# Cutting the POOL subtraction of each weight unit into two instructions of 512 columns in place of four of 256

## The reference

```
def swiglu(h, w_in, w_out):
    gate, up = jnp.split(h @ w_in, 2, axis=-1)
    return (jax.nn.silu(gate) * up) @ w_out
...
        x = x + 0.5 * swiglu(rms_norm(x, norm_ffn1_w[l]), ffn1_w_in[l], ffn1_w_out[l])
        x = x + hybrid_mixer(rms_norm(x, norm_mix_w[l]), w_in_mix[l], conv_w[l], conv_b[l], ...)
        x = x + memory_cross_attention(rms_norm(x, norm_cross_w[l]), rms_norm(mem, norm_mem_w[l]), ...)
        x = x + 0.5 * swiglu(rms_norm(x, norm_ffn2_w[l]), ffn2_w_in[l], ffn2_w_out[l])
```

## Time and profile before

| | |
|---|---|
| median of 3 runs | 2134.8 us (2134.48 to 2135.26) |
| span of the profiled execution | 2133.4 us, first to last instruction |
| PE busy | 2114.8 us, 99% |
| DVE busy | 829.8 us, 39% |
| ACT busy | 803.6 us, 38% |
| POOL busy | 1120.5 us, 53% |
| `w_lo` instructions on POOL | 1448 of 128x256, mean 783 ns |
| granted PE clock | 1.000 of full speed |

### The profile page before, as it was taken

The page is one execution under the profiler, slowest core; times in us unless marked ns, Lnnn a source line. Parts: engine busy times, 40 slices in busy tenths (PEclk is TensorE's granted clock), DMA queues, the critical chain, the costliest instruction groups (busy, mean ns, idle before and its releaser), DMA issues.

```text
span 2133.4 us, 29164 instructions
## 1 busy us (share of the span) xinstructions
PE 2114.8 (99%) x10122; PEld 1740.7 (82%) x10122; DVE 829.8 (39%) x1489; ACT 803.6 (38%) x1345; POOL 1120.5 (53%) x1493
## 2 busy tenths in 40 slices
PE   9999999999999999999999999999999999999999
PEld 7888888878887778877888888887787888888887
DVE  5222211762841766143322222208744474023244
ACT  5222232325834655323322223326554343122233
POOL 6555555673354337725655555554545466555554
PEclk9999999999999999999999999999999999999999
DMA  6322233233322213412332223321222223332322
GB/s 214 119 98 98 99 106 106 85 99 96 114 99 79 75 55 122 155 40 89 99 98 98 95 94 117 99 96 63 79 89 79 89 80 108 99 99 99 99 89 80
DMA packets 61344, 207.71 MB, mean 97 GB/s; under 512 B 6616, under 2 KB 8088, under 8 KB 61256
## 3 DMA queue, kind: packets, MB, share of 16 engines
q1 hardware_dynamic: 55216, 195.84, 27.8%
q10 hardware_dynamic: 6040, 10.65, 1.5%
HBM read 204.31 MB, written 4.77 MB: 98 GB/s over the span
## 4 chain that ended last, share of the span: by engine, by line
PE 42%; issue 28%; POOL 27%; DVE 2%; POOLq 0%; ACT 0%; DMA 0%; SPq 0%; DVEq 0%; ACTq 0%
POOL w_lo L463 27%; PE bank L516 11%; PE bank L518 11%; PE bank L517 11%; PE bank L678 1%; PE bank L680 1%; PE bank L679 1%; PE bank L908 1%; PE bank L932 1%; PE bank L840 1%; PE bank L920 0%; DVE gx_lo L2394 0%; DVE bank L2403 0%; PE bank L846 0%; DVE x L2405 0%
## 5 line engine op out<-in xcount | busy, mean ns | idle before, releaser
L463 POOL TENSOR_TENSOR w_lo<-w_raw,w_hi 128x256 fp32r<-128x256 f32 x1448 | 1087.1, 783 | 933.4 <-ACT w_hi L1283 933.3
L516 PE MATMUL bank<-gx_hi,w_hi 128*128 128x512 f32 (+1 forms) x1768 | 674.9, 382 | 7.8 <-DVE gx_lo L2394 4.5
L518 PE MATMUL bank<-gx_hi,w_lo 128*128 128x512 f32 (+1 forms) x1768 | 668.1, 378 | 0.0
L517 PE MATMUL bank<-gx_lo,w_hi 128*128 128x512 f32 (+1 forms) x1768 | 667.6, 378 | 0.0
L1283 ACT CAST w_hi<-w_raw 128x1024 fp32r<-128x1024 f32 x364 | 378.4, 1045 | 347.9 <-PE bank L518 291.8
L516 PEld LDWEIGHTS bank<-gx_hi,w_hi 128*128 128x128 f32 x1768 | 332.6, 188 | 74.2 <-DVE gx_lo L2394 6.4
L518 PEld LDWEIGHTS bank<-gx_hi,w_lo 128*128 128x128 f32 x1768 | 332.5, 188 | 62.1
L517 PEld LDWEIGHTS bank<-gx_lo,w_hi 128*128 128x128 f32 x1768 | 332.7, 188 | 60.5 <-issue 0.2
L516 PE MATMUL bank<-ff_hi,w_hi 128*128 128x512 f32 x352 | 136.9, 389 | 0.0
L517 PE MATMUL bank<-ff_lo,w_hi 128*128 128x512 f32 x352 | 136.9, 389 | 0.0
L518 PE MATMUL bank<-ff_hi,w_lo 128*128 128x512 f32 x352 | 136.9, 389 | 0.0
(11 more groups left out here) (358 smaller groups left out, 2703.4 us busy)
## 6 DMA issues: line engine op xcount, KB each, us to landing
w_raw<-wstream SPq DMA_DIRECT2D x364, 512.0 KB, 3.5
bias_spread<-bias_rows ACTq DMA_DIRECT2D x1, 2560.0 KB
square<-cum_rows ACTq DMA_DIRECT2D x8, 256.0 KB, 3.5
rfin_row<-cum_rows ACTq DMA_DIRECT2D x8, 256.0 KB, 3.1
outT<-ple_o SPq DMA_DIRECT2D x8, 256.0 KB, 2.0
x<-xT SPq DMA_DIRECT2D x3, 512.0 KB, 8.0
square<-bias_spread ACTq DMA_DIRECT2D x4, 256.0 KB, 2.6
rfin_row<-bias_spread ACTq DMA_DIRECT2D x4, 256.0 KB, 2.7
```

The lines of the kernel that those rows point to most:

```text
L463: ins = nc.gpsimd.tensor_tensor(w_lo[:, s, part], w_raw[:, s, part], w_hi[:, s, part].bitcast(F32), ALU.subtract)
L516: nc.tensor.matmul(dst, hi, rhs[0], start=first, stop=False)
L517: nc.tensor.matmul(dst, hi, rhs[1], start=False, stop=False)
L518: return nc.tensor.matmul(dst, lo, rhs[0], start=False, stop=last)
```

## The change

`split_unit` cuts a unit's 1024 columns into two parts of 512 in place of four of 256. The four `proj` units near the end, of which only the first 512 columns are used, take one instruction in place of two. The waits and the addition to `unit_lo` stay where they are: one wait ahead of the unit, one addition behind its last instruction.

```diff
@@ -456,10 +456,10 @@
-            def split_unit(r, s, parts=4):
+            def split_unit(r, s, parts=2):
                 pool.wait_ge(unit_hi, r * RING + (s + 1))
                 for q in range(parts):
-                    part = slice(q * UNIT // 4, (q + 1) * UNIT // 4)
+                    part = slice(q * UNIT // 2, (q + 1) * UNIT // 2)
                     ins = nc.gpsimd.tensor_tensor(w_lo[:, s, part], w_raw[:, s, part], w_hi[:, s, part].bitcast(F32),
                                                   ALU.subtract)
                 ins.then_inc(unit_lo, 1)
@@ -504,7 +504,7 @@
             for u in range(UNIT0["proj2a"], UNITS):
-                split_unit(u // RING, u % RING, parts=2 if u in PROJ_UNIT.values() else 4)
+                split_unit(u // RING, u % RING, parts=1 if u in PROJ_UNIT.values() else 2)
```

## The result

The changed kernel takes 2149.97 us (median of 5 runs, 2149.78 to 2150.82), the kernel before 2134.80 (5 runs, 2134.43 to 2135.26): 15.2 us slower, ratio 1.0068 with the 95% interval [1.0057, 1.0079]. The forecast was 2141.0 us, from 2133.5 to 2144.5. The direction was right, the size less than half of the measured one, and the time lies outside the range. The profiled execution spans 2148.2 us, 14.8 more than before.

What follows compares the result with a forecast made beforehand. PE bounds the kernel, busy 2114.8 of 2133.4 us. Terms 0.85 + 2.2 + 2.5 + 0.4 + 0.2 = 6.15 us on 2133.4, plus 1.4 from span to median, gave 2141.0 us; 8-in-10 range 2133.5 to 2144.5.

Steps and rivals of the forecast that it cites:

- A: Whole kernel: POOL's longer turn at the shared reads reaches PE through DVE; 2141.0 us, own range 2137.5 to 2145, chance 0.62.
- B: Whole kernel: the turn does not depend on the instruction's length, so time stays 2134.8 us within 1.5; chance 0.20.
- C: Scan and end of `mix_attn`: a fixed part of the turn is paid once, not twice; 2132.3 us, chance 0.08.
- the end of `mix_attn`: Chain to `kx_T`: seven units at two turns each, 0.8 us felt per turn; 2.5 us more, bounds 0.5 to 3.5.
- POOL's instruction and the ring: POOL: 512 columns take 1.22 us, a unit 2.44 for 2.82, hidden; the next DMA starts 0.4 us sooner, gaining nothing.
- The size of the turn: POOL's hold on the port against DVE: 0.45 to 0.5 us before, 0.9 to 1.0 after, taken as 1.0.
- the scan's cell: Scan, DVE's instructions before `q_T`: stretched 1.65 us, 0.5 more than before; 2.2 us over five units, bounds nothing to 3.
- Hidden by one bank of room: Convolution: DVE needs 5.7 us a tile against PE's 5.44; 4 us lag over 16 tiles, hidden by 4.7 us of room.
- rival E: Convolution: the lag exceeds its room and PE waits for a bank or `w_lo`; 1 to 3 us more, 2143, chance 0.03.
- Rival D: Stall for `kx_T` grows to about 4 us and the clock falls; 3 us more, 2144, chance 0.07.
- the stick-breaking attention: Stick-breaking attention: 0.2 us lost at its first `stick_lo`.
- The opening: Opening: later `gx_lo` chunks are delayed, up to 0.85 us at the fourth; cost 0.85 us, bounds 0.3 to 1.1.

Runs made afterwards that it cites:

- e4: Kernel before, with 512 columns in 236 units outside the opening, convolutions, scan, end of `mix_attn`, gates and starts by halves: 2135.39 us, ratio 1.0002.
- the four partial kernels: Kernel before, with 512 columns only at the convolution, scan, end of `mix_attn`, or opening, gates and halves: 2139.10, 2138.64, 2140.83, 2138.72 us.
- e8: Kernel before, POOL unchanged, with DVE's PSUM-reading copy to `m_row` before `kx_T` run seven times in place of once: 2140.26 us, ratio 1.0021.
- e1: Kernel before, with every weight unit subtracted in eight instructions of 128 columns in place of four of 256: 2142.77 us, ratio 1.0033.
- e7: Kernel before, POOL unchanged, with DVE's PSUM-reading copy to `m_row` before `kx_T` run four times in place of once: 2138.01 us, ratio 1.0012.
- e5: Kernel before, with each weight unit subtracted in one instruction of 1024 columns (512 for units from `proj2a` on): 2171.87 us, ratio 1.0168.

## Why the prediction was right or wrong

**The mechanism (A) was right.** The longer turn reaches PE through DVE. B (not a matter of the length) is rejected by e4 together with the four partial kernels and by the row of the convolution at four widths. C needs a turn with a fixed part, and there is next to none: 0.55, 1.11 and 2.23 us for 256, 512 and 1024 columns. What is there once for each turn is DVE's free 0.3 us, and fewer turns mean fewer of these, so C had the sign the wrong way. The prediction had this in words ("Two long turns are felt more fully") and in one term, the end of `mix_attn`, where it left about 0.2 us of each turn unfelt; it priced the convolution's tile without saying how. The signs that it named came, most of them larger: `gx_lo` of the opening at 1.77 us (1.7 forecast), `state` at 1.51 (1.4), the wait for `kx_T` at 3.9 (4), for `q_T` at 3.2 (2.5).

The section on the chip says that the engines meet only through semaphores. The stretched rows show that this is not so: POOL and DVE also meet, without a semaphore, where both read SBUF.

**POOL's instruction and the ring** were as said: 1.25 us and more in place of the 1.22 forecast, 2.55 us a unit in place of 2.44, hidden everywhere.

**The size of the turn** is the step that failed first. The text took "the turn of POOL" as 0.45 to 0.5 and 0.9 to 1.0 us. It is 0.55 and 1.1: `sumsq` at 1.22 us in the earlier trace rows already showed 0.55 over its 0.68, `gx_lo` in the changed kernel shows 1.11. On the scan's cell this alone is the difference: 1.65 us were forecast and 1.84 came (0.75 for `y_b`, 1.09 for `state`) against 1.1 before, so the steps were 0.7 and not 0.5.

**"Hidden by one bank of room"** is the step that cost most. The lag of the convolution was set to nothing, and it cost 3.3 us. For the convolution 5.7 us a tile was forecast and a lag of 4 us under 4.7 of room. `conv_in` of the changed kernel starts every 5.86 us in the mean (391.82 to 468.00, 13 steps), 0.42 above PE's 5.44. Over 16 tiles that is 6.7 us, 2.0 more than the room, and PE lost 2.2. A difference of 0.16 us a tile, about what two turns 0.1 too short each make, decided between nothing and a loss. What was left of the lag came out behind the stage, at a wait of which the prediction has no word (1.15 us at `dt_T`):

```profile
474.92 0.39 PE L805 MATMUL bank<-consts,dt_T 16*128 16x16 f32 x4 [1.11 <-DVE dt_T L1949]
```

This is rival E's mechanism, which had a chance of 0.03 and 1 to 3 us; it came with 3.3.

**The clock** is the second miss. Rival D named the stall, its length (about 4 us; 3.94 measured) and 3 us of price, but at a chance of 0.07, and as an alternative to A. It is no alternative: the forecast itself lengthened this stall to about 4 us. If A holds, D's condition holds. e8 shows that such a stall lowers the clock without POOL's longer instructions; the price was 2.2 us in the changed kernel.

**Places not looked at.** `cc_t` and the stick-breaking attention cost 1.7 us where 0.2 was forecast. The kernel before already had both as waits for DVE, and that of `cc_t` was as long as that of `q_T`, which the prediction did price. Its list of the largest waits left out `cc_t` and also `ff_silu` (1.6 us, unchanged):

```profile
PE bank L516 <- DVE cc_t L2262: 0.6, 1, 0.6
...
PE bank L1146 <- DVE stick_lo L2331: 0.2, 1, 0.2
```

The opening (0.85 forecast, 0.85 measured) and the gain on `w_lo` in the starts by halves, taken up by `gx_lo`, were right; the first start lost 1.1 us where 0.2 was forecast.

In sum, 8.6 us were missing, in rounded terms: 3.3 in the convolution, 2.2 of the clock, 0.9 in the scan, 0.8 up to `kx_T`, 1.5 at `stick_lo` and `cc_t` and 0.8 in the starts by halves, less 0.6 at `branch2` and 0.2 before it.

## What to carry to other kernels

When two engines exclude each other by whole instructions, the loss of the one, where it works back to back, is (turn - its own pause) for each instruction of the other: cut the other's instructions until the turn fits into the pause, and do it only where the first is in somebody's way, since smaller instructions cost their own engine time (a unit took POOL 3.35 us in e1 in place of 2.82). A lag that is "hidden by a buffer" must be worked out to a tenth of a microsecond a tile before it is set to zero, because 16 tiles multiply it; and what is left of it must be followed past the end of the stage. If a forecast lengthens a stall of PE, the clock behind the stall belongs in the same case, not in a rival.

## What the runs showed of the hardware

- A POOL subtraction of 128, 256, 512 columns is followed by the next after 0.42, 0.70 and 1.25 to 1.28 us: about 2.2 ns a column and 0.14 us fixed. Of that, 2.15 to 2.2 ns a column hold up a DVE instruction with both operands in SBUF, up to 2.23 us in one piece with 1024 columns. The Trainium skill ("SBUF — State Buffer", "Who interferes with whom") says that such a DVE instruction contends with a GpSimd instruction that reads SBUF, and gives no size for it; the runs agree.
- With 128 columns such turns cost back-to-back DVE instructions nothing (median 752 ns against 751 undisturbed), with 256 0.25 us, with 512 0.80, with 1024 1.90.
- Line 1938, with one tile read from SBUF, is stretched as well by instructions of POOL that overlap with it: median 682 ns in e1 against 547.
- `conv_in`, which reads PSUM and SBUF, takes 0.69 us beside POOL and without it.
- The granted clock fell to half within or behind stalls of PE of 3.9 and 4.1 us, whether DVE's copies or POOL's turns had made them, and was full again 4.4 to 4.9 us after their end. Behind one of 2.7 us (e7) it held in the profiled execution, and behind one of 2.0 us (e5) it fell. It also fell among the short stalls of the first start by halves, in some executions and not in others.
